# Eight experts in rising order of their token counts: five of 80 slots, then two of 96

## The reference, cut to what matters

```python
logits = (xt @ w_router).astype(jnp.float32)      # xt: 256 x 1024, 8 experts
top_v, top_e = lax.top_k(logits, TOP_K)           # TOP_K = 2
gates = jax.nn.softmax(top_v, axis=-1)
...
def _swiglu(x, w1, w3, w2):
    return (jax.nn.silu(x @ w1) * (x @ w3)) @ w2  # 1024 x 3584, twice, and 3584 x 1024 for each expert
```

## Time and profile before

| what | us |
|---|---|
| median of 3 runs (lowest, highest) | 3237.35 (3237.31, 3238.67) |
| span of the profiled execution | 3237.5 |
| from the first up product of the experts to their last line 819 product | 869.15 |

### The profile page before, as it was taken

One profiled execution on the slowest core, in us unless ns is written; L12 is line 12 of the kernel. 1 busy time (PEld: TensorE's weight loads), 2 busy tenths in 40 slices (PEclk: granted clock), 3 DMA queues, 4 the chain that ended last, 5 costly groups with the idle time before them and its releaser, 6 DMA issues.

```text
span 3237.5 us, 76009 instructions
## 1 busy us (share of the span) xinstructions
PE 3185.4 (98%) x34760; PEld 2616.3 (81%) x34760; DVE 1049.5 (32%) x2232; ACT 409.6 (13%) x1027; POOL 50.5 (2%) x86
## 2 busy tenths in 40 slices
PE   9999999999999999999998999999999999999999
PEld 6685985777699999999997967588895976688894
DVE  2252564043201101111013661211566562210465
ACT  1240000042111000000001001210100001110100
POOL 0000000000000000000000000000000000000000
PEclk9999999999999999999998999999999999999999
DMA  7423444323699999999996444334444444434442
GB/s 255 151 98 154 182 159 172 144 107 124 240 392 358 360 418 385 426 427 426 427 426 252 172 160 171 130 130 156 157 164 162 181 150 171 155 111 149 157 177 90
DMA packets 63091, 714.11 MB, mean 221 GB/s; under 512 B 7568, under 2 KB 9232, under 8 KB 11888
## 3 DMA queue, kind: packets, MB, share of 16 engines
q1 hardware_dynamic: 59328, 703.62, 55.6%
q0 software_dynamic: 1008, 5.94, 0.5%
q10 hardware_dynamic: 2624, 2.65, 0.4%
HBM read 709.30 MB, written 1.05 MB: 219 GB/s over the span
## 4 chain that ended last, share of the span: by engine, by line
PE 94%; DMA 3%; DVE 1%; ACT 1%; issue 0%; POOL 0%; SPq 0%; POOLq 0%; DVEq 0%; ACTq 0%
PE psum L599 50%; PE psum L790 15%; PE psum L720 10%; PE psum L800 7%; PE psum L855 5%; DMA weight_ring<-in_experts 3%; PE psum L819 1%; PE psum L1152 1%; PE psum L765 1%; PE psum L637 1%; PE psum L633 1%; PE psum L886 1%; PE psum L632 0%; POOL statistics L521 0%; PE psum L1126 0%
## 5 line engine op out<-in xcount | busy, mean ns | idle before, releaser
L599 PE MATMUL psum<-arena,weight_ring 128*128 128x256 f32 (+1 forms) x5408 | 974.3, 339 | 7.6 <-DVE arena L2071 3.8
L599 PEld LDWEIGHTS psum<-arena,weight_ring 128*128 128x128 f32 x5408 | 869.5, 191 | 98.1 <-issue 14.3
L790 PE MATMUL psum<-arena,weight_ring 128*64 128x80 f32 (+2 forms) x14336 | 565.5, 237 | 7.9 <-issue 3.3
L790 PEld LDWEIGHTS psum<-arena,weight_ring 128*64 128x64 f32 x14336 | 542.8, 137 | 17.4 <-issue 9.0
L599 PE MATMUL psum<-weight_ring,arena 128*128 128x128 f32 (+3 forms) x3024 | 511.2, 326 | 2.0 <-DVE arena L1841 2.0
L599 PEld LDWEIGHTS psum<-weight_ring,arena 128*128 128x128 f32 x3024 | 385.9, 192 | 113.9 <-issue 106.8
L800 PE MATMUL psum<-arena,weight_ring 128*64 128x80 f32 (+2 forms) x7168 | 300.1, 237 | 3.0 <-issue 3.0
L1729 DVE TENSOR_TENSOR arena<-arena,psum 128x80 f32<-128x80 f32 (+2 forms) x224 | 54.5, 243 | 716.3 <-ACT arena L1319 716.3
L800 PEld LDWEIGHTS psum<-arena,weight_ring 128*64 128x64 f32 x7168 | 280.4, 137 | 3.6 <-issue 3.6
L855 PE MATMUL psum<-weight_ring,arena 128*128 128x512 f32 x384 | 168.6, 597 | 0.0
L1319 ACT ACTIVATE arena<-psum 128x80 f32<-128x80 f32 (+2 forms) x224 | 54.4, 243 | 744.3 <-PE psum L790 744.3
(11 more groups left out here) (265 smaller groups left out, 1999.4 us busy)
## 6 DMA issues: line engine op xcount, KB each, us to landing
weight_ring<-in_experts SPq DMA_DIRECT2D x224, 1536.0 KB, 12.0
weight_ring<-in_ffn_up SPq DMA_DIRECT2D x44, 2048.0 KB, 7.8
weight_ring<-in_second_wide SPq DMA_DIRECT2D x42, 2048.0 KB, 7.7
weight_ring<-in_first_wide SPq DMA_DIRECT2D x35, 2048.0 KB, 8.8
weight_ring<-in_ffn_down SPq DMA_DIRECT2D x20, 2048.0 KB, 7.7
weight_ring<-in_dense_up SPq DMA_DIRECT2D x11, 2048.0 KB, 7.8
weight_ring<-in_dense_down SPq DMA_DIRECT2D x5, 2048.0 KB, 7.8
weight_ring<-in_ffn_down SPq DMA_DIRECT2D x4, 1024.0 KB, 5.0
```

What stands on the lines that cost most here:

```text
L599: m = pe.matmul(o, lhs, rhs, start=i == 0, stop=i == len(terms) - 1)
L790: mm = pe.matmul(psum[g * STRIP:(g + 1) * STRIP, q % 4, m * CAP:m * CAP + tokens], w[:, m, k, g * STRIP:(g + 1) * STRIP], chosen[:, k, 0:t ...
```

## The change

The order behind the first expert becomes one of rising counts, and the tiers become 96 slots for place 0, 80 for places 1 to 5, and 96 for places 6 and 7. The width of 88 is gone. The gather at the end of an expert always makes 96 columns; before it made as many as the expert that was ending had slots. The key of expert 0 changes its sign, so that it stays first. For the counts above the widths meet these counts: 96 for 64; 80 for 41, 45, 66, 69 and 73; 96 for 76 and 78. The general path is as it was.

```diff
 CAP = 3 * SEQ * 2 // EXPERTS // 2
 SMALL_CAP = 5 * SEQ * 2 // EXPERTS // 4
-FULL = 3
-MIDDLE = 2
-MIDDLE_CAP = 11 * SEQ * 2 // EXPERTS // 8
-TIERS = ((0, MIDDLE, CAP), (MIDDLE, FULL, MIDDLE_CAP), (FULL, EXPERTS, SMALL_CAP))
+LARGE = 2
+TIERS = ((0, 1, CAP), (1, EXPERTS - LARGE, SMALL_CAP), (EXPERTS - LARGE, EXPERTS, CAP))
...
-                gather(e + 1, tokens)
+                gather(e + 1, CAP)
...
-                    v.tensor_tensor(greater, keys..., keys..., ALU.is_gt).then_inc(once["slotted"].sem, 1)
+                    v.tensor_tensor(greater, keys..., keys..., ALU.is_lt).then_inc(once["slotted"].sem, 1)
...
-                               repeated(np.append([2.0 * SEQ], np.arange(EXPERTS - 2, -1, -1) / EXPERTS).astype(np.float32)),
+                               repeated(np.append([-2.0 * SEQ], np.arange(EXPERTS - 2, -1, -1) / EXPERTS).astype(np.float32)),
```

More of the change, by code:

```diff
@@ L2012, in _ @@
                     dve.wait_ge(*once["slotted"].by(0, 5))
-                    v.tensor_tensor(greater, keys.unsqueeze(1).broadcast_to(square), keys.unsqueeze(2).broadcast_to(square), ALU.is_gt).then_inc(once["slotted"].sem, 1)
+                    v.tensor_tensor(greater, keys.unsqueeze(1).broadcast_to(square), keys.unsqueeze(2).broadcast_to(square), ALU.is_lt).then_inc(once["slotted"].sem, 1)
                     dve.wait_ge(*once["slotted"].by(0, 6))
```

## The result

The changed kernel takes 3247.08 us (median of 7 runs, 3246.15 to 3248.09) against 3237.90 us for the kernel before (7 runs, 3237.31 to 3239.38). The ratio is 1.0027, with a 95% interval of 1.0017 to 1.0037. So it is slower by 9.2 us; 10.5 had been forecast. A second series gave 3247.03 us, 8.6 more than the kernel before in it (3238.43), ratio 1.0027, 1.0016 to 1.0038. One of the 15 executions of the kernel before in that series ran at a lower clock (0.849 instead of 0.996) and took 3679.94 us; it is left out of every comparison.

What follows compares the result with a forecast made beforehand. TensorE was taken to pace 96-slot experts and weight loads the 80-slot ones. Width 9.17, gather 0.43 and entries 0.9 gave 10.5 us on 3237.35, so 3247.9 us; the 8-in-10 range was 3243.8 to 3254.

Steps and rivals of the forecast that it cites:

- The width, 9.17 us: Place 2's expert of 88 slots is replaced by a third of 96: 9.17 us without stalls, all on the path.
- Five narrow experts, no cost for the move: The five 80-slot experts move from places 3 to 7 to places 1 to 5, still 516.9 us: cost 0.
- No late load in the wide experts at the end: Places 6 and 7 start with an almost empty ring of loads, yet no load is late in place 6: cost 0.
- One gather of 0.43 us: Gathers of 96 columns end places 1 to 5; only the one ending place 5 counts, +0.43 us.
- Entry stalls, +0.9 us: TensorE's stalls on entering tiers: 1.5 us at place 0, 4.1 at place 1, 3.5 at place 6; net +0.9 us.
- the rival of cheap entries: Place 6 entered at 1.5 us, place 1 at 2.6: stalls -2.6, total +7.0; it shares 81% with the forecast.
- The dear entry: At place 6 all six instruction fetches stall 1.79 us each: 10.7 us rather than 3.5, total +17.7; chance 12%.
- Vector and scalar work, 0: VectorE's comparison and the constant's sign replace same-size instructions; ScalarE and VectorE are mostly idle in the experts: 0.
- The clock behind the experts, 0 within -1.7 to +3: Behind the experts, a shifted half-level clock could change TensorE's work by -1.7 to about +3 us; taken as 0.
- loads never late in the narrow experts: The ring lasts through five narrow experts at 100.76 us each, giving back 9.0 us: total +1.5; chance 4%.
- loads pace the wide experts too: Loads set the pace in 96-slot experts, so the width swap costs nothing: total +0.9 us; chance 2%.
- A narrow expert of 101 us: Sign that the prediction is wrong: narrow experts in places 1 to 5 taking 101 us, against about 102.1 to 104.9 expected.

Runs made afterwards that it cites:

- width run: Kernel before with 96 slots instead of 88 in place 2, falling order and three tiers kept: 3245.7 us against 3237.99, ratio 1.0023.
- two-tier run: Kernel before with 96 slots in place 2 and places 0 to 2 sharing one loop: 3245.47 us, ratio 1.0024.
- wide gathers: Kernel before with gathers of 96 columns at the end of every expert, nothing else: 3238.2 us, ratio 1.0003.
- order: Rising order with all widths of the kernel before kept, which needs four tiers: 3241.73 us, ratio 1.0011 to the kernel before.
- changed kernel again: The changed kernel run once more without any edit, for a second profile: 3247.03 us.

## Why the prediction was right, point by point

The forecast was 10.5 us, and 9.2 (8.6 in the second series) were measured. The direction and the main term held. That the size came so close is in part luck, as the sum below shows.

1. *The width, 9.17 us.* Right. The unstalled wide expert took 119.11 us in place 1 of the width run, in places 1 and 2 of the two-tier run, and 119.16 and 119.13 in place 7 of the changed kernel's two profiles. The width alone gave +7.7 us, with an entry cheaper by 1.3.

2. *Five narrow experts, no cost for the move.* Right, with some luck in the size. The changed kernel's five sum to 514.7 us against 516.9 before. The runs in falling order gave 515.5 (wide gathers), 515.9 (width) and 514.7 (two tiers), and those in rising order 515.7 (order) and 515.2 (changed kernel again). The order isn't what separates them, and before's profile had the highest sum of them. I took one execution's sum as fixed, though it holds an entry that varies.

3. *No late load in the wide experts at the end.* Right. Though it follows experts that the loads paced, place 6 shows no wait for experts' weights, and neither does place 7. The idle gaps inside its rounds are those of the entry.

4. *One gather of 0.43 us.* Agrees with the total, but is too small to be confirmed by it. Its place was wrong: I had expected 103.7 us in place 5, and it took 103.3, as the other load-paced places did. The sum below counts the 0.43 at place 1 instead.

5. *Entry stalls, +0.9 us.* This is the term that was mis-sized most. The three entries of the changed kernel came to 5.95 and 6.5 us against 8.2 in before's profile, so -2.2 and -1.7. I had put place 1 at 4.1 and it took 2.8 and 3.1; place 6 at 3.5 and it took 2.8 and 2.3; place 0 kept as 1.5 and took 0.3 and 1.1. So the rival of cheap entries, with -2.6, was nearer here than the forecast: place 1 came close to its 2.6, while place 6 lay between its 1.5 and my 3.5. The dear entry, 10.7 us at place 6, didn't come. But the fear behind it wasn't empty: a narrow entry in load-paced time cost 6.3 us. The wider unit left less idle time between two restarts (0.8 us a gap against 1.2 to 1.6 in the rows shown).

6. *Vector and scalar work, 0.* Nothing in the profiles speaks against it: VectorE is busy 1049.6 us against 1049.5.

7. *The clock behind the experts, 0 within -1.7 to +3.* It was +0.4.

The profile's sum closes: 9.17 (width) + 0.43 (gather at place 1) - 2.2 (entries) - 1.35 (places 2 to 5, 410.7 against 412.1) = 6.0, beside 6.1 measured. So against the profile that its terms were read from, the forecast was over 4 us too high, 3.1 of them in the entries. One more mistake stands apart from these terms. I added to the median as if the profiled span of before were at it. About 1.5 us lie around every span, so before's profiled execution was most likely slower than its median, by 1.1 us. Its dear entries may explain this in part. Measured from a slower execution than usual, the profile's difference is too small, and this is most likely why 10.5 lies nearer to the medians' 9.2 than to 6.1. Against the profile of the run with wide gathers, which has before's tiers but took 1.9 us less than its median, the changed kernel's eight stretches sum to 7.6 and 8.3 us more.

Of the other rivals, "loads never late in the narrow experts" and "loads pace the wide experts too" both fell by the stretches: 103.3 us at a share of 1.01 in places 4 and 5, and 119.1 at 0.93 in place 1 of the width run. The second would have followed from the Trainium skill's 358 GB/s for one core ("DMA: Bandwidth & Descriptors", "Specifications"); this core, alone on the chip, moved 426 in every load-paced stretch. A narrow expert of 101 us was to be a sign against the prediction, and place 2 took 101.3 in both profiles; but it was the only one, and lived on stock as before's place 4 did with 102.1. The general path wasn't taken, or the eight stretches wouldn't be there. The Trainium skill's rule that instructions come in blocks of 16 KiB ("Runtime: NRT & Kernel Launch", "Instruction fetch mechanics") held up better: one tier fewer took five packets of 16 KB away, one tier more brought six.

What stays open in part is why an entry costs 0.5 us in one stage and 6.3 in another. With a full ring it was 0.5, 1.0 and 1.3 us at 96 slots, 2.6 and 2.9 at 88, and 2.8 to 4.1 at 80. Behind load-paced experts it was 2.1 to 2.8 us at 96 slots, 4.6 at 88, and 6.3 at 80. Place 0 fits neither row well, with 0.3 to 2.8 us at 96 slots and 5.3 at 80. The effect of the width is shown by the restarts: they come about every 6 us whatever the width, and narrower steps fill less of that. That busy DMA engines make the packets late is an argument from these rows, and no run varied that alone; nor does any show why place 0 varies so much.

## What to carry to other kernels

Cut the trace at the loop's own boundaries and ask for each pass which side paced it. The price of a wider pass is then simple (0.04 us for each slot and unit here), and it counts in full only where the other side doesn't pace. An average over the whole phase, with TensorE 99% busy and a DMA share of 0.97 before the change, would have shown neither.

Before a loop is cut in variants to save work, count the first pass through each new body as a cost of its own, and expect it to be dearest where the body's steps are short; here that was also where the DMA engines were saturated. And compare an execution's profile with its own time: terms of 1 to 3 us taken from one profile can't be better than executions agree.

## What the runs showed of the hardware that was not expected

- Each further tier in the code brings five or six packets of 16 KB on the instruction queue: 90, 96, 101 and 107 packets for one, two, three and four tiers, and none for places 1 and 2 in the two-tier run, which pass again through the loop that place 0 entered.
- Inside an entry TensorE's stops lie 127 or 128 products apart, and the restarts after them 5.0 to 6.5 us, most of them 5.8 to 6.4, at 80, 88 and 96 slots alike.
- A stall of TensorE in a load-paced stage isn't free: of 6.3 us, 4.1 were covered, by the waits for loads of two experts, and 2.2 stayed.
- The same entry to the same code varies by 0.3 to 0.8 us between two executions of one kernel, and the entry to the wide place 0 by 2.5 us over nine profiles.
